# Ten of eleven down projections in seven products of half-size blocks instead of eight

## The reference, cut to what matters

```
gate, up = jnp.split(xf @ w_ffn_in, [D_FF], axis=-1)
h = h + rms_norm((jax.nn.silu(gate) * up) @ w_ffn_out, n_ffn_post)
```

## Time and profile before

| | us |
|---|---|
| median of 3 runs | 1212.9 |
| lowest | 1210.0 |
| highest | 1925.83 |
| profiled execution, its own time | 1212.49 |
| its span | 1210.7 |
| TensorE busy in the span | 1179.2 (97%) |
| VectorE busy | 741.2 (61%) |
| GpSimd busy | 422.9 (35%) |
| ScalarE busy | 409.4 (34%) |

### The profile page before, as it was taken

One profiled execution on the slowest core, in us unless ns is written; L12 is line 12 of the kernel. 1 busy time (PEld: TensorE's weight loads), 2 busy tenths in 40 slices (PEclk: granted clock), 3 DMA queues, 4 the chain that ended last, 5 costly groups with the idle time before them and its releaser, 6 DMA issues.

```text
span 1210.7 us, 21798 instructions
## 1 busy us (share of the span) xinstructions
PE 1179.2 (97%) x8411; PEld 1157.4 (96%) x8411; DVE 741.2 (61%) x1203; ACT 409.4 (34%) x718; POOL 422.9 (35%) x304
## 2 busy tenths in 40 slices
PE   7999999999999998799999999999999999999997
PEld 6999999999999986699999999999999999999997
DVE  5559899944455247965555555655656565656556
ACT  5444444333344245531313131313131313222223
POOL 3066788213122267431313132322222222222226
PEclk9999999999979999899999999999999999999999
DMA  9211111121144233121212020202011121212134
GB/s 311 87 35 53 35 53 53 36 72 36 36 139 114 88 122 116 44 71 36 71 35 69 17 87 0 88 16 86 18 59 45 40 64 35 69 35 69 36 143 173
DMA packets 99797, 84.49 MB, mean 70 GB/s; under 512 B 2722, under 2 KB 89378, under 8 KB 99738
## 3 DMA queue, kind: packets, MB, share of 16 engines
q1 hardware_dynamic: 99554, 83.61, 22.4%
q10 hardware_dynamic: 192, 0.17, 0.0%
HBM read 72.86 MB, written 11.38 MB: 70 GB/s over the span
## 4 chain that ended last, share of the span: by engine, by line
PE 91%; POOL 3%; DVE 3%; issue 2%; DMA 1%; ACT 1%; DVEq 0%; ACTq 0%; POOLq 0%
PE ps L356 28%; PE ps L358 28%; PE ps L357 28%; PE ps L1756 1%; POOL o_last L690 1%; POOL h_ring L663 1%; PE ps L1582 1%; PE ps L1621 1%; PE ps L1686 1%; PE ps L1705 1%; PE ps L1810 1%; PE ps L1809 1%; DMA t_sm<-table_identity_decays 1%; POOL st L546 1%; DVE w_ring L1409 1%
## 5 line engine op out<-in xcount | busy, mean ns | idle before, releaser
L356 PE MATMUL ps<-xn_hi,w_hi 128*128 128x350 f32 (+2 forms) x576 | 187.2, 325 | 0.3 <-DVE xn_lo L1114 0.2
L358 PE MATMUL ps<-xn_lo,w_hi 128*128 128x350 f32 (+2 forms) x576 | 185.2, 322 | 0.0
L357 PE MATMUL ps<-xn_hi,w_lo 128*128 128x350 f32 (+2 forms) x576 | 184.9, 321 | 0.0
L356 PE MATMUL ps<-x_hi,w_ring 128*128 128x256 f32 x616 | 174.2, 283 | 7.2 <-DVE w_ring L1409 6.3
L356 PE MATMUL ps<-x,w_ring 128*128 128x260 f32 x616 | 175.4, 285 | 1.6 <-issue 1.2
L357 PE MATMUL ps<-x,w_ring 128*128 128x260 f32 x616 | 175.3, 285 | 0.0
L358 PE MATMUL ps<-x,w_ring 128*128 128x260 f32 x616 | 175.0, 284 | 0.0
L358 PE MATMUL ps<-x_lo,w_ring 128*128 128x256 f32 x616 | 173.6, 282 | 0.0
L357 PE MATMUL ps<-x_hi,w_ring 128*128 128x256 f32 x616 | 173.5, 282 | 0.0
L356 PE MATMUL ps<-act_hi,fx_hi 128*128 128x388 f32 (+1 forms) x528 | 171.3, 324 | 0.3
L358 PE MATMUL ps<-act_lo,fx_hi 128*128 128x388 f32 (+1 forms) x528 | 168.5, 319 | 0.0
(11 more groups left out here) (232 smaller groups left out, 2496.4 us busy)
## 6 DMA issues: line engine op xcount, KB each, us to landing
f_raw<-in_w_ffn_in SPq DMA_DIRECT2D x42, 512.0 KB, 4.2
raw<-in_w_in SPq DMA_DIRECT2D x24, 512.0 KB, 3.9
f_raw<-in_w_ffn_out SPq DMA_DIRECT2D x22, 512.0 KB, 3.3
x_st<-in_x_prompt SPq DMA_DIRECT2D x8, 512.0 KB, 7.9
raw<-in_w_out SPq DMA_DIRECT2D x8, 512.0 KB, 5.6
h_ring<-in_x_prompt SPq DMA_DIRECT2D x8, 512.0 KB, 4.6
h_scratch<-h_ring SPq DMA_DIRECT2D x8, 512.0 KB, 3.0
h_fin<-h_scratch SPq DMA_DIRECT2D x8, 512.0 KB
```

The lines of the kernel that those rows point to most:

```text
L356: nc.tensor.matmul(out, hi, mhi, start=first, stop=False, skip_group_check=resumes)
L357: nc.tensor.matmul(out, lo, mhi, start=False, stop=False, skip_group_check=resumes)
L358: return nc.tensor.matmul(out, hi, mlo, start=False, stop=last, skip_group_check=resumes)
```

## The change

Groups 0 to 9 do the down projection in seven products too. Output features are halved (mh), tokens are halved (nh, 516 each), and the two blocks of 128 features are the inner halves. The order is p = 0, 1, 3, 2, 4, 6, 5. A product has four tiles of 128 output features by 516 tokens, a tile lies in two PSUM banks (258 columns each), and all eight banks are used. Products 0 to 3 of the list accumulate onto each other in PSUM, 4 and 5 as well, and 6 stands alone: VectorE adds the running sum to one quadrant of `ffn_acc` after every product. Group 10 keeps the plain form, with its weights now in ring slots.

The weights of the seven products go through the same ring, now 7 slots, and the lookahead is 6 products instead of 3. So a group has 21 products. GpSimd gets a third `w_sums` per group, four sums of activation halves (`act_sum_3` to `act_sum_6`), the multiplication that was the second half of `act1` for e = 1, seven low parts of activations instead of four, and three low parts of weights (k = 20, and k = 0 and 1 of the next group).

```diff
-RING = 4
-AHEAD = 3
+MIX_RING = 4
+RING = 7
+AHEAD = 6
+MIX_AHEAD = 3
+CATCH_UP = {7: (10, 11), 8: (12, 13), 9: (14, 15), 10: (16,), 11: (17,), 12: (18,), 13: (19,)}
+QUAD = HALF // 2
+DOWN_P = (0, 1, 3, 2, 4, 6, 5)
+DOWN_QUADRANT = ((0, 0), (1, 0), (0, 1), (1, 1), (1, 1), (0, 0), (1, 0))
+DOWN_ACT = (0, 2, 3, 1, 0, 1, 2)
+ACT_COUNT = (1, 4, 3, 2, 5, 7, 6)
...
+        def w_ops_at(k, first, last):
+
+            if first:
+                return (k + MIX_AHEAD,) if k < 7 else CATCH_UP[k]
+            return (k + AHEAD,) if k + AHEAD < (14 if last else 20) else ()
+
+        def lo_ready(eng, g, k, first=False):
+
+            if k == 20:
+                eng.wait_ge(s_plo, 3 * g + 1)
+            elif k in (0, 1) and not first:
+                eng.wait_ge(s_plo, 3 * g - 1 + k)
+            else:
+                eng.wait_ge(s_olo, splits(g, k))
+        def raw_pair(e):
+
+            return ((0, 1), (2, 0), (1, 2))[e]
...
SP, ffn_loads:
-                    sp.wait_ge(s_olo, 14 * g + 7)
+                    sp.wait_ge(s_olo, splits(g - 1, 13))
                     load_gate_up(0, g, 0, 0)
-                    sp.wait_ge(s_fxlo, 2 * g - 1)
+                    sp.wait_ge(s_olo, splits(g - 1, 19))
+                    load_gate_up(2, g, 1, 0)
+                    sp.wait_ge(s_plo, 3 * g - 2)
                     load_gate_up(1, g, 0, 1)
-                    sp.wait_ge(s_fxlo, 2 * g)
-                    load_gate_up(2, g, 1, 0)
                     sp.wait_ge(s_olo, splits(g, 5))
                     load_gate_up(0, g, 1, 1)
                     sp.wait_ge(s_olo, splits(g, 6))
-                    load_down(1, g, 0)
+                    load_down_half(1, g, 0)
                 sp.wait_ge(s_olo, splits(g, 12))
-                load_down(2, g, 1)
+                load_down_half(2, g, 1)
...
GpSimd, one group:
+                w_sums(gg, 1)
+                act_lo_of(gg, 1, 0, e_s2[:, :])
+                act_sum_3(gg, first)
+                pool.wait_ge(s_asum, 4 * gg + 1)
+                act_lo_of(gg, 2, 1, x_diff)
+                w_sums(gg, 2)
+                act_sum_4(gg)
+                act_lo_of(gg, 3, 3, e_s3[:, :])
+                pool.wait_ge(s_asum, 4 * gg + 2)
+                act_lo_of(gg, 4, 2, x_diff)
+                act_sum_5(gg, first)
+                act_1(gg)
+                act_sum_6(gg)
+                w_op_lo(gg, 20)
+                pool.wait_ge(s_asum, 4 * gg + 4)
+                act_lo_of(gg, 5, 0, side(first))
+                act_lo_of(gg, 6, 2, x_diff)
+                w_sums(gg + 1, 0)
...
GpSimd, end of w_sums; act_lo_of(.., 7, ..) lies inside it for e = 0:
+                elif not first:
+                    act_lo_of(gg - 1, 7, 1, e_s2[:, :])
+                    w_op_lo(gg, 0)
+                    pool.wait_ge(s_plo, 3 * gg - 1)
+                g.tensor_tensor(t4, gate[:, half:D], t2, ALU.subtract).then_inc(s_T, 1)
+                if e == 0 and not first:
+                    w_op_lo(gg, 1)
...
ScalarE, beside the down products j:
+            def down_step(g, j, first):
+
+                if j == 0:
+                    w_op_hi(g, 20)
+                else:
+                    w_op_hi(g + 1, j - 1)
+                if j == 0:
+                    act_hi_sum(g, 3, 0, side(first), 1)
+                elif j == 1:
+                    act_hi_sum(g, 4, 2, x_diff, 2)
+                elif j == 2:
+                    act.wait_ge(s_down, 28 * g + 12)
+                    act.wait_ge(s_p1, 4 * g + 4)
+                    act_hi_of(1, e_s2[:, :])
...
VectorE:
+                up1(g, 1, first, 13)
+                for j in range(7):
+                    mh, nh = DOWN_QUADRANT[DOWN_P[j]]
+                    for pos, i in enumerate(tile_order(j)):
+                        dve.wait_ge(s_down, 28 * g + 4 * j + pos + 1)
+                        a = ffn_acc[:, 4 * mh + i, nh * HALF:(nh + 1) * HALF].rearrange("p (a n) -> p a n", a=2)
...
+                            v.tensor_tensor(a, tile_banks(i), a, ALU.add).then_inc(s_acc, 1)
+                for k in range(2, AHEAD):
+                    w_op_lo(g + 1, k)
...
TensorE:
+            def down_product(g, j):
+
+                p = DOWN_P[j]
+                a = DOWN_ACT[p]
+                lo_ready(pe, g, 14 + j)
+                pe.wait_ge(s_alo, 7 * g + ACT_COUNT[p])
+                w_hi_k, w_lo_k = w_slot(14 + j, 0), w_slot(14 + j, 1)
+                for i in tile_order(j):
+                    if j == 0:
+                        for done in ((s_s3, s_c21) if i < 2 else (s_sga, s_c12)):
+                            pe.wait_ge(done, 4 * g + 3 + i % 2)
+                    else:
+                        pe.wait_ge(s_acc, 28 * g + 4 * (j - 1) + i + 1)
+                    kc = slice(i * P, (i + 1) * P)
+                    for n in range(2):
+                        c = slice(n * QUAD, (n + 1) * QUAD)
+                        ins = three_pass(tile_banks(i)[:, n, :], w_hi_k[:, kc], w_lo_k[:, kc],
+                                         act_hi[:, a, c], act_lo[:, a, c], p in (0, 4, 5), True, p not in (0, 4, 5))
+                    ins.then_inc(s_down, 1)
```

More of the change, by code:

```diff
@@ L294, in w_op @@
         def w_op(k, first):
[L296 to L299, removed]
+            e, p = part_of(k)
+            gate, up = (f_raw[:, r, :] for r in raw_pair(e))
             t3, t2, t4 = f_sum[:, 0, :], f_sum[:, 1, :], gate[:, 0:D // 2]
@@ L334, in w_slot @@
         def w_slot(k, part):
-            return w_ring[:, k % RING, part, :]
+            return w_ring[k % MIX_RING if k < 0 else k % RING][:, part, :]
         CREDIT_AB = 6
@@ L640, in w_sums @@
                 pool.wait_ge(s_T, 4 * i + 3)
-                if not first:
[L642 to L651, removed]
+                if e:
+                    pool.wait_ge(s_olo, splits(gg, 7 * e))
+                elif not first:
+                    act_lo_of(gg - 1, 7, 1, e_s2[:, :])
+                    w_op_lo(gg, 0)
+                    pool.wait_ge(s_plo, 3 * gg - 1)
@@ L991, in w_op_hi @@
                     act.wait_ge(s_wojob, 3 * SLOTS + 9)
-                elif first or k >= RING:
+                elif first and k < MIX_RING:
+                    act.wait_ge(s_pd, products(g, k - MIX_RING, 1, first))
+                elif first and k < RING:
+                    act.wait_ge(s_h, 9)
+                    act.wait_ge(s_hs, 9)
+                elif k < RING:
+                    act.wait_ge(s_down, 28 * (g - 1) + 4 * (k + 1))
+                else:
                     act.wait_ge(s_pd, products(g, k - RING, 1, first))
@@ L1032, in product_step @@
                 if p == 5:
[L1033 to L1036, removed]
+                    if last:
+                        act.wait_ge(s_down, 28 * g)
                         act_hi_half(g, e, 1)
+                    elif e == 1:
+                        act_hi_half(g, 1, 1)
                     gate1_silu(g, e, first, k)
+                if k == 13 and not last:
+                    act_hi_sum(g, 2, 2, x_diff, 0)
+            def down_step(g, j, first):
+                if j == 0:
+                    w_op_hi(g, 20)
+                else:
+                    w_op_hi(g + 1, j - 1)
[7 more added lines that the diff above has]
+                    act_hi_of(1, e_s2[:, :])
             act.wait_ge(s_wlo, SLOTS + N_IN + N_OUT)
@@ L1061, in ffn_group @@
                 for k in range(14):
[L1062 to L1067, removed]
+                    product_step(g, k, first, last)
+                if last:
+                    act_hi_half(g, 1, 0)
+                else:
+                    for j in range(7):
+                        down_step(g, j, first)
             ffn_group(0, first=True)
@@ L1429, in u3, with act2 @@
                     v.tensor_tensor(e_s1[:, c], ps[:, 5 + 2 * ss, 0:SUBW[ss]], e_s3[:, c], ALU.add).then_inc(s_c21, 1)
-            def act2(g, e, first, k):
+            def act2(g, e, first, k, last):
+                dst = e_s3 if e or last else side(first)
                 for ss in subs_of(first, k):
@@ L1470, in product_step @@
                 if p == 4:
-                    act2(g, e, first, k)
-                if k in (8, 12):
-                    down_w_lo(g, (k - 8) // 4)
+                    act2(g, e, first, k, last)
+                if k in (10, 12) and last:
+                    down_w_lo(g, (k - 10) // 2)
             for t in range(12):
@@ L1531, in ffn_group @@
                     c0, n = DOWN_CHUNKS[c]
-                    dve.wait_ge(s_down, 24 * g + j + 1)
+                    dve.wait_ge(s_down, ACC_LAST + j + 1)
                     a = ffn_acc[:, m, c0:c0 + n]
[L1534 to L1542, removed]
+                    v.tensor_tensor(a, ps[:, 4 + j % 4, 0:n], a, ALU.add).then_inc(s_acc, 1)
+                    if j == 2 * KT:
+                        dve.wait_ge(s_acc, ACC_LAST + j)
                         for a in range(2):
@@ L1557, in _ @@
                 ffn_group(i)
-            ffn_group(NG - 1, last=True)
```

(5 more changed lines are left out.)

244 lines of the change are left out of this document (168 added, 76 removed).

## The result

The changed kernel takes 1183.39 us (median of 4 runs, 1181.33 to 1184.58) against 1212.08 for the kernel before in the same set; the ratio of their runs is 0.9769, 95% interval 0.9756 to 0.9781. One run of the kernel before took 1925.83 us; it is far off the other three (1210.0 to 1212.9) and is left out of the ratio. The forecast was 1185, range 1180 to 1205. The profiled execution of the changed kernel took 1184.2 us, its span 1182.4.

A forecast was written before the change was run, and what follows sets the result against it. TensorE's stream of matmul starts was taken to bound the kernel. 1212.49 - 30.6 (ten shorter down stages) + 2.3 (waits before the seventh gate product) = 1184.2 profiled; 1184.6 for the median, said as 1185, range 1180 to 1205.

The forecast's parts named there:

- What bounds it: In groups 0 to 10, time is the number of matmuls times the distance of their starts, until another engine is late.
- The price of 258 columns: On TensorE, 168 matmuls of 258 columns at 0.1188 us, 19.95 a down stage against 23.01; gain 3.06 us a group.
- Group 0: Group 0 has eight operands to catch up; GpSimd's list ends about 1 us later against T, inside 2.2 us.
- T: End of the 14th product of a group, 915.45 in the rows, from which GpSimd's times are counted.
- the prediction's own last sentence: Wrong if TensorE waits outside two chains: GpSimd's to the last down product, the one to the seventh gate product.
- The rule against the change: Skill page's mostly per-instruction matmul price, 98 ns at 258 columns, 115 at 388: a loss of 0.7 us a group, 1220.
- VectorE's adds: 28 down-stage adds of 516 columns, 0.70 us each, 0.61 in a row, against TensorE's 0.71 a tile; path cost nothing.
- GpSimd's chain: Before the last down product: weight 20 split T+5.4, load T+9.6, t2 T+12.2, seventh low part T+14.9; 2.2 us spare.
- The seventh product: Gate product k=6 waits for act2's bank, freed at S+17.1, S being the group's start, wanted S+17.25; 2.3 us in all.
- A: GpSimd instructions all stretch to 1.75 us beside two-SBUF-input VectorE work: 3.2 us a group, 1213; in full and beyond 0.08.
- B: A's stretch in both chains, and VectorE's splits 9, 10 held by GpSimd: 3.7 us more a group, 1246; chance 0.04.
- C: Matmuls priced by count, 0.137 us each at 258 columns: nothing gained, 1213, or 1220 at the page's proportions; chance 0.02.

The follow-up runs named there:

- the two versions without gaps: Kernel before with weight splits moved behind adds: cut into 192 matmuls of 258 columns, 1209.81 us; with its own 144 tiles, 1206.36 us.
- The first cut version: Kernel before with the plain down projection of groups 0 to 9 cut into 192 matmuls of 258 columns instead of 144: 1241.06 us.
- the yardstick: The changed kernel run once more, unaltered, against the kernel before: 1183.06 us, ratio 0.9778.

## Why the prediction was right

**What bounds it.** Right: the distance of matmul starts, at an unchanged clock, sets the time in both kernels.

**The price of 258 columns.** 0.1188 us foreseen, 0.1195 measured; 19.95 against 20.07 a stage. The gain of the stage was 2.94 instead of 3.06 in the nine groups of the loop, 1.1 us less in all.

**Group 0.** It gained 2.6 instead of 3.06. The 0.34 that TensorE waited for the add of `up1` is a wait that neither chain contains; by the prediction's own last sentence it was wrong there, though for 0.34 us of 28. The low part of GpSimd ended 1.6 us later against T than in the loop, where 1 was foreseen; it just held.

**The rule against the change.** The figures cited from the Trainium skill ("TensorE: Matmul & The Clock Gate", Back-to-back issue gap) give, as an estimate, 3.1 us a group for 48 more matmuls of the same total columns; the two versions without gaps measured 0.3 (22.90 and 22.60). For this stream of fp32r pairs the trace does not agree with the page. The first cut version shows how nearly a total time can confirm a wrong theory.

**VectorE's adds.** Foreseen 0.70 alone and 0.61 in a row; measured 0.696 and 0.60. The cover named was the true one: four copies more cost at most 2 us, seven some 11.

**GpSimd's chain.** Foreseen T + 5.4, 9.6, 12.2 and 14.9; measured T + 5.8, 10.0, 12.7 and 15.4. The 0.4 came in at the low part of 837.15, which started at T - 1.1 as foreseen and took 1.75 instead of 1.3 beside VectorE's work. Sum 4 before it started 0.4 late and took 1.69, but that was absorbed. Slack 1.8 instead of 2.2.

**The seventh product.** The chain S + 3.4, 7.55, 10.65, 13.3, 14.7 and 17.1 was measured as 3.3, 7.9, 10.55, 13.5, 14.9 and 17.2. The mechanism was right, its cost over-sized: 2.3 us foreseen, 0.56 in the profile after and 1.3 in that of the yardstick. Against the profile after that is 1.7 too much, while the price of 258 columns and group 0 are 1.6 too little. So the agreement to the tenth, 1184.2 foreseen for the profiled execution and 1184.2 measured, is luck; that the parts were each right within 2 us is not.

**The rivals.** A (all given back): its premise, every instruction stretched to 1.75, did not occur. In a group of the loop four of GpSimd's 27 instructions were stretched: sum 4 to 1.69, one low part to 1.75 and the t4 of two `w_sums` to 1.54. The others stayed at 1.3. B needed GpSimd busy while VectorE split weights 9 and 10; they took 0.69 and 0.68. C is refuted by the down stage itself, 168 matmuls in 20.07 us, 0.1195 each. That a multiplication which GpSimd took over would have cost VectorE far more than 0.4 us was in no rival; at 4 to 5 us it is the strongest effect found of the two engines working side by side.

## What to carry to other kernels

Price a matmul by the distance of starts at its own width, then ask which waits the shorter stage uncovers: a stage that shrinks per tile makes other engines' waits show that four banks used to bridge. Follow each in-order engine list to the instruction that TensorE waits for and put the slack in numbers; the sums here were right within 0.5 us in the loop, but group 0, written out, had a third of the loop's slack. When an experiment's time matches a theory, look at its trace before believing it: 1241 us were foretold for one reason and came for another.

## What the runs showed of the hardware that was not expected

GpSimd's addition with one SBUF operand as both inputs took 1.04 us for 512 columns (2.04 for two in a row), against 1.29 with two different ones. One of VectorE's multiplications with two SBUF inputs took 1.53 us instead of 0.42 beside GpSimd, while its adds from PSUM kept 0.60 in a row beside the same engine. A PSUM bank that came free 0.05 us before its matmul was due still cost TensorE 0.2; the weight load for it had been due 0.06 before the bank was free.
